# Even mixer of a two-block network: gated result left in PSUM, and four moves in the orders of the engines

## The reference, cut to what matters

```
z = h @ w_in                                  # u, v (4 x 128 each), q, k, vv (8 heads x 64), 8 gate logits
u, v = gelu(z[u]), rms_norm(gelu(z[v]))       # per group of 128
y_a = u * (W_s v + b)                         # W_s: 128 x 128 per group, the "spatial product"
log_f = log_sigmoid(f_logit + b_f);  c = cumsum(log_f)
logits = rms_norm(q) . rms_norm(k) / 8 + c[t] - c[s],  causal
y_b = softmax(logits) @ vv
y = concat(y_a, y_b) @ w_out
```

## Time and profile before

| | |
|---|---|
| time, median of 3 runs (lowest, highest) | 1989.06 us (1986.73, 1989.92) |
| the profiled execution's own time, its span | 1989.65 us, 1987.6 us |
| PE busy | 1916.0 us, 96% of the span |
| DVE, ACT, POOL busy | 975.3, 705.1, 922.9 us |
| granted TensorE clock, mean | 0.988 |
| the mixer with its output projection | about 706 to 914 us of the span |

### The profile page before, as it was taken

The page is one execution under the profiler, slowest core; times in us unless marked ns, Lnnn a source line. Parts: engine busy times, 40 slices in busy tenths (PEclk is TensorE's granted clock), DMA queues, the critical chain, the costliest instruction groups (busy, mean ns, idle before and its releaser), DMA issues.

```text
span 1987.6 us, 23051 instructions
## 1 busy us (share of the span) xinstructions
PE 1916.0 (96%) x8775; PEld 1572.0 (79%) x8775; DVE 975.3 (49%) x1267; ACT 705.1 (35%) x1038; POOL 922.9 (46%) x414
## 2 busy tenths in 40 slices
PE   7999789999999999999899999999999899999999
PEld 5777588888888877787778888888788778888887
DVE  6865875544431248546564444311955564444301
ACT  4544343322323345544443232222234543232221
POOL 3564544545444434635425444544445435444542
PEclk9999899999999999999999999999999999999999
DMA  4232112332322322103223233233333223323222
GB/s 151 85 109 77 43 43 85 106 106 84 105 95 93 100 85 85 64 22 114 78 64 106 90 100 105 77 98 106 106 106 106 85 64 106 96 94 106 80 95 79
DMA packets 165064, 178.91 MB, mean 90 GB/s; under 512 B 4584, under 2 KB 152544, under 8 KB 164737
## 3 DMA queue, kind: packets, MB, share of 16 engines
q1 hardware_dynamic: 161996, 172.08, 27.1%
q10 hardware_dynamic: 2997, 5.84, 0.9%
HBM read 175.82 MB, written 2.10 MB: 90 GB/s over the span
## 4 chain that ended last, share of the span: by engine, by line
PE 58%; issue 20%; POOL 10%; DVE 6%; ACT 3%; SPq 1%; POOLq 0%; DMA 0%; DVEq 0%; ACTq 0%
PE acc L524 18%; PE acc L526 17%; PE acc L525 17%; POOL w_lo L2219 9%; PE aux L524 1%; PE aux L525 1%; PE aux L526 1%; PE aux L599 1%; PE aux L656 1%; ACT w_hi L1770 1%; DVE ye_lo L1116 0%; SPq L454 0%; DVE c_lo L1116 0%; DVE a_lo L1121 0%; PE acc L873 0%
## 5 line engine op out<-in xcount | busy, mean ns | idle before, releaser
L2219 POOL TENSOR_TENSOR w_lo<-w_raw,w_hi 128x1024 fp32r<-128x1024 f32 x326 | 803.2, 2485 | 926.9 <-ACT w_hi L1770 926.9
L524 PE MATMUL acc<-a_hi,w_hi 128*128 128x512 f32 (+1 forms) x1480 | 583.0, 394 | 5.7 <-POOL w_lo L2219 3.9
L525 PE MATMUL acc<-a_lo,w_hi 128*128 128x512 f32 (+1 forms) x1480 | 578.0, 391 | 0.0
L526 PE MATMUL acc<-a_hi,w_lo 128*128 128x512 f32 (+1 forms) x1480 | 577.7, 390 | 0.0
L1770 ACT ACTIVATE w_hi<-w_raw 128x1024 fp32r<-128x1024 f32 x326 | 327.2, 1052 | 445.3 <-PE acc L526 419.2
L524 PEld LDWEIGHTS acc<-a_hi,w_hi 128*128 128x128 f32 (+1 forms) x1480 | 278.2, 188 | 74.1 <-issue 8.4
L526 PEld LDWEIGHTS acc<-a_hi,w_lo 128*128 128x128 f32 (+1 forms) x1480 | 278.2, 188 | 59.4
L525 PEld LDWEIGHTS acc<-a_lo,w_hi 128*128 128x128 f32 (+1 forms) x1480 | 278.2, 188 | 59.3 <-issue 1.4
L524 PE MATMUL acc<-h_hi,w_hi 128*128 128x512 f32 x528 | 205.8, 390 | 0.0
L526 PE MATMUL acc<-h_hi,w_lo 128*128 128x512 f32 x528 | 205.4, 389 | 0.0
L525 PE MATMUL acc<-h_lo,w_hi 128*128 128x512 f32 x528 | 205.4, 389 | 0.0
(11 more groups left out here) (409 smaller groups left out, 2432.7 us busy)
## 6 DMA issues: line engine op xcount, KB each, us to landing
w_raw<-in_w_gate SPq DMA_DIRECT2D x22, 1024.0 KB, 5.1
w_raw<-in_w_up SPq DMA_DIRECT2D x22, 1024.0 KB, 5.1
w_raw<-in_w_down SPq DMA_DIRECT2D x16, 896.0 KB, 5.1
w_raw<-in_hy_w_in SPq DMA_DIRECT2D x12, 1024.0 KB, 5.0
w_raw<-in_ffn_w_gate SPq DMA_DIRECT2D x11, 1024.0 KB, 5.2
w_raw<-in_ffn_w_up SPq DMA_DIRECT2D x11, 1024.0 KB, 5.1
w_raw<-in_e_w_in SPq DMA_DIRECT2D x10, 1024.0 KB, 5.0
w_raw<-in_xa_wkv SPq DMA_DIRECT2D x8, 1024.0 KB, 5.0
```

Source lines behind the costliest of these rows:

```text
L524: nc.tensor.matmul(o, l_hi, r_hi, start=start, stop=False)
L525: nc.tensor.matmul(o, l_hi, r_lo, start=False, stop=False)
L526: return nc.tensor.matmul(o, l_lo, r_hi, start=False, stop=stop)
L2219: nc.gpsimd.tensor_tensor(w_lo[s][:, half], w_raw[s][:, half], w_hi[s][:, half].bitcast(F32), ALU.subtract)\
```

## The change

Five edits, all in the mixer of this one layer:

1. The product with u is written back to its PSUM bank instead of `u_t`. ACT reads `ye_hi` from the bank and DVE reads the bank for `ye_lo`, which now frees the bank. DVE does group 3 right after group 2, ahead of the normalization of q.
2. The spatial products go before tile 3 of q0 instead of tile 2, and the transposes of q go before tile 1 of k1 instead of between k0 and k1.
3. ACT splits v0 before it copies the four tiles of `q_hi`, not after.
4. ACT splits out1 after the first of the four value tiles, not after the last. After the third it does an Exp on one column that nobody reads.
5. O of the pair before comes after the first scores of a pair's successor (qt 0) instead of after the second (qt 1), on all engines. It waits for the transposed probabilities of its later query tiles only when it comes to them.

```diff
-            if p and qt == 1:
+            if p and qt == 0:
                 order.append(("O", p - 1, 0))            # both in fox_steps and in fox_vector_steps
...
-        token_blocks(a_hi, a_lo, TT, name="q", inside=gmlps)
+        token_blocks(a_hi, a_lo, TT, name="q", inside=gmlps, at=(0, 3))
...
-        token_blocks(a_hi, a_lo, TT, name="k", between=lambda: head_transposes("q", q_raw))
+        token_blocks(a_hi, a_lo, TT, name="k", inside=lambda: head_transposes("q", q_raw), at=(1, 1))
...
         def mixed_values(p):
-            aux_result(("T", p, TT - 1, 1))
+            aux_result(("T", p, 1, 0))
...
             for i in range(2):
...
+                if i == 1:
+                    aux_result(("T", p, TT - 1, 1))
...
-            free_aux(V.tensor_tensor(u_t[:, g, :], bank, u_t[:, g, :], ALU.mult), again=True)
+            for_act(V.tensor_tensor(bank, bank, u_t[:, g, :], ALU.mult))
+            spatial_banks.append(bank)
...
         def spatial_low(g):
             acted()
-            halve(ye_hi[:, g, :], ye_lo[:, g, :], u_t[:, g, :], last=step)
+            halve(ye_hi[:, g, :], ye_lo[:, g, :], spatial_banks[g], last=free_aux)
...
         spatial_gate(2)
+        spatial_gate(3)
         normalized_heads(q_raw, 0, 2)
         spatial_low(2)
         normalized_heads(q_raw, 2, 4)
-        spatial_gate(3)
         spatial_low(3)
...
         def spatial_high(g):
-            act.wait_ge(aux_free, mark[("gmlp", g)] + 1)
-            result(S.activation(ye_hi[:, g, :], u_t[:, g, :], ACT.Copy))
+            given()
+            result(S.activation(ye_hi[:, g, :], aux[:, mark[("gmlp", g)] % 4, :], ACT.Copy))
...
         spatial_high(3)
+        split_next()
         heads_high("q", q_hi, small[:, 1:2])
-        split_next()
         raw_squares("k", k_raw, 0, 4)
...
             result(ins_)                                  # v_hi of tile t
+            if t == 0:
+                split_next()
+            if t == 2:
+                S.activation(gate_log[:, 0:1], gate_log[:, 1:2], ACT.Exp)
         evac.next(TT)
-        split_next()
```

More of the change, by code:

```diff
@@ L553, in wide_block, with token_blocks @@
             block_done(outs)
-        def token_blocks(l_hi, l_lo, tiles, name=None, between=None, inside=None):
+        def token_blocks(l_hi, l_lo, tiles, name=None, between=None, inside=None, at=None):
             banks = []
@@ L560, in token_blocks @@
                 for t in range(tiles):
-                    if inside and (b, t) == (0, 2):
+                    if (b, t) == at:
                         inside()
@@ L1456, in spatial_gate @@
                                         par("e_g_v_2", g), bs_bc[:, g:g + 1, :].to_broadcast([P, TT, P]), ALU.mult, ALU.add))
-            free_aux(V.tensor_tensor(u_t[:, g, :], bank, u_t[:, g, :], ALU.mult), again=True)
+            for_act(V.tensor_tensor(bank, bank, u_t[:, g, :], ALU.mult))
+            spatial_banks.append(bank)
+        spatial_banks = []
         def spatial_low(g):
             acted()
-            halve(ye_hi[:, g, :], ye_lo[:, g, :], u_t[:, g, :], last=step)
+            halve(ye_hi[:, g, :], ye_lo[:, g, :], spatial_banks[g], last=free_aux)
         def by_head(ap):
```

## The result

The kernel after takes 1992.99 us (median of 20 runs, 1990.13 to 1994.84). The kernel before, run on the same chip between them, takes 1989.12 us (median of 20, 1986.73 to 1990.63). The ratio is 1.0018, with an interval from 1.0011 to 1.0024. So the change costs 3.9 us, just inside the 4 us that were called no change, and 2.9 us more than the forecast of 1990.1.

A forecast was written before the change was run, and what follows sets the result against it. TensorE was taken as the bound (busy 96%), so gains could come only from its idle or low-clock time. Terms +2.15 + 3.2 - 4.35 = +1.0 us took the median from 1989.06 to 1990.1, range 1981.5 to 1994.5.

The forecast's parts named there:

- likeliest case: Whole kernel: the forecast itself, +1.0 us to a median of 1990.1, own range 1987 to 1993, chance 0.50.
- second rival: First scores and last pair: lower clock through all first scores and again in the last pair, +4.5, 1993.6; chance 0.20.
- Spatial products earlier: TensorE before the spatial products in q0: the stall goes, -2.25 us with nothing late on DVE.
- `decays` under POOL: DVE's `decays`: POOL's k0 block stops line 1450, so it ends 4.3 us later; bounds 0 and 4.3.
- first rival: Front: `decays` isn't stopped by POOL, front -6.5, total -7.6, 1981.5 us; chance 0.20.
- The chain to q's transposes: DVE's stops delay q's normalization: product at 784.6, TensorE idle 7.0 us instead of 4.85; +2.15 up to v0.
- the low clock stays as it was: Behind the stall before q's transposes: the low clock unchanged, as the idle stretch exceeds the one that brought it.
- Edit 4: First scores: out1's early split waits for v1, `v_hi` stands behind, first Exp at L + 7.25; +3.2, bounds +2.2 and +5.2.
- third rival: First scores: out1's early split isn't held by v1, first Exp 1.8 us earlier, total -4.0, 1985.1 us; chance 0.05.
- Edit 5: Pair products: O covers the waits for exponentials, and the last pair keeps full clock; -4.35 us, bounds -2.9 and -4.7.

The follow-up runs named there:

- x3: The kernel after with `decays` done behind k's normalization and the unread Exp on another column: 1984.41 us, 0.9975 of the kernel before.
- x1: The kernel after with out1 split after the last value tile again, the unread Exp kept: 1987.22 us, 0.9993 of the kernel before.
- z3: The kernel before, unchanged, run once more for a second profile: one run of 1988.1 us, span 1986.1.
- y4: The kernel before with only out1's split moved after the first value tile and the unread Exp added: 1993.34 us, 1.0021 of the kernel before.
- z1: The kernel before with only the first three edits (product left in PSUM, spatial products and q's transposes moved, v0 split early): 1991.00 us, ratio 1.0009.
- x4: The kernel before with only the product left in its PSUM bank and group 3 ahead of q's normalization: 1988.02 us, 0.9992 of the kernel before.
- y1: The kernel after with `decays` behind k's normalization and out1 split after the last value tile, unread Exp kept: 1979.38 us, 0.9950 of the kernel before.
- x2: The kernel after with v0 split after the four `q_hi` copies again: 1989.39 us, 0.9999 of the kernel before.
- y3: The kernel before with only the unread Exp added after the third value tile: 1988.54 us, 0.9997 of the kernel before.
- y2: The kernel before with only O of the pair before moved behind the successor's first scores: 1984.57 us, 0.9980 of the kernel before.
- z2: The kernel after with late `decays`, out1 split after the last value tile and v0 split after `q_hi`: 1977.41 us, 0.9941 of the kernel before.

## Why the prediction was right, and what was sized wrong

**Kind and range.** No change within 0.2% was the likeliest, and the ratio is 1.0018. The time lies in the range, at the edge of the likeliest case's own (1987 to 1993), and nearer to the second rival's 1993.6 than to 1990.1. That it still counts as no change has some luck in it: 3.9 us stand against a bound of 4, the interval reaches 4.8, and two of the three terms were too low.

**Spatial products earlier.** Right: the idle before them is gone.

**`decays` under POOL.** Right in mechanism and size: 4.3 us predicted, 2.25 and 2.09 measured. In the profile of the kernel after one of the two stops fell on another instruction than named, a copy with one SBUF input (L1450 there, 2.67 us, 8 partitions; the two that were named are its L1452). The Trainium skill (SBUF - State Buffer, "Who interferes with whom") lists `tensor_scalar` among the operations that can take the pair of ports shared with GpSimd when their operands meet its conditions, beside those with two SBUF inputs; the row agrees. The first rival, with this stop at zero, is refuted by these rows. x3 shows its price: without `decays` in the way front and time fall by 9.5 and 8.6 us.

**The chain to q's transposes.** Product at 784.6 predicted, 784.13 measured; idle 7.0 and 6.70. The failed sentence is "the low clock stays as it was": of the matmuls behind the stall 5.5 us ran at the lower clock (784.19 to about 789.7), where 3.3 did before. At half a microsecond each that is 1.1 more, less 0.3 for the shorter idle: +3.0 measured for a term of +2.15. This is the first mis-sized term, and its upper bound of +3 was just reached. x1 bears this out: with the same stall and 6.8 us at the lower clock, of which 2.9 lie on matmuls, its front is 1.3 us shorter. The measured +3.0 is also against the one profile that was read; against z3's front it is +5.6.

**Edit 4.** Right in mechanism: the split waits for v1, `v_hi` stands behind it, idle of 3.98 and 1.02 us (3.75 and 1.2 predicted), first Exp at L + 7.16 (7.25 predicted). x1 and y4 show this cause from both sides, and refute the third rival. The value taken, +3.2, was too low: +4.66 in two profiles. That value assumed part of the first scores at full clock. In the kernel after and in y4 all of them ran at the lower one, the assumption of the upper bound (+5.2), and z1 prices this without edit 4's wait at 0.95 us (third scaling at L + 11.63 instead of 10.68). So by these rows the term is 3.7 plus 0.95. This is the second mis-sized term.

**The second rival** was half right: the lower clock over all first scores came, the one in the last pair didn't. But that the longer idle after L brings it isn't shown. All four profiles with the early split have at least 10.2 us of it; so do x4, z1 and y1 without the early split, and x1 has none. What decides it stays open.

**Edit 5.** -4.35 predicted, -4.44 in the whole, -4.45 alone (-4.7 by medians). The 1.01 us stall left the clock at full, as taken.

**The sum.** 2.15 + 3.2 - 4.35 = +1.0 was predicted, 3.0 + 4.66 - 4.44 = +3.2 was measured in the profile. The medians differ by 3.9. The 0.7 beyond isn't broken down; z3 shows that executions of the kernel before differ by 2.6 us in front, so one profile is no better a base than that. Nor do the parts add up by medians: 1.2 + 4.1 - 4.7 = +0.6, against +3.9 together. Their four intervals, added by squares, are about 3.4 us wide to either side (an estimate), so this gap of 3.3 us may be noise or may be that the edits act on each other; it isn't shown which. z1's profiled run lies 1.85 us above its median (1992.85 and 1991.00), so its usual front is likely shorter than in its profile and in that of the kernel after. Which executions take which course was not resolved.

## What to carry to other kernels

Before an instruction is moved ahead in a queue, look at what it waits for: if that is the end of the same work that the queue should attend to, all behind it now waits as well, and the move is a loss (4.1 us here) whatever it was to give. When a stop between two engines is taken away at one instruction, ask which instruction will lie under the same block at its new time; here the 4.3 us passed from `ye_lo` to `decays`, and with `decays` off the way the front was shorter than in both executions of the kernel before (by 3.9 and 6.5 us), which it was in none of z1, x1, x2 and the kernel after. Where a kernel has two courses, profile it twice before a term of a few microseconds is built on one trace.

## What the runs showed of the hardware that was not expected

- The same idle of 2.08 us before the same 32 matmuls was followed by the full clock in two executions (the kernel before as shown, y3) and by 3.4 us at the lower one in four (z3, x4, y2, y4). An idle of 1.0 to 1.1 us in the pairs (852.26 before, 869.89 after) was followed by the full clock each time it was looked at; the one of 1.32 us in the last pair by 3.4 us at the lower clock in the kernel before, by 6.8 in y4, and by none in z1 and y3.
- Time at the lower clock can cost less than half of itself. Where it fell into idle time of TensorE it cost nothing (the fronts of x1, z1 and the kernel after, above), and over the first scores, where TensorE also waits for POOL and ACT, little. Three kernels with the same instructions in the tail (x1, z2, y1) had 0, 6.8 and 13.6 us of it and tails of 64.51, 65.06 and 66.30 us: 1.8 us for 13.6.
- The stop of a DVE instruction under a GpSimd one doesn't shrink with its size: 8 partitions of 512 stood 2.25 us longer than alone, 128 of 16 about 2.1 us, where POOL worked at halves of 2.4 us. It fell on two instructions of DVE for each block of two halves, while the product of the spatial gate, with one input in PSUM, took 0.69 us in the midst of one.
